# Three chained blocks on one core: gates, decays and sums of block 2 reordered, five norms taken by token columns, tokens chosen from PSUM

## The reference, cut to what matters

```python
def reference(x, ...):
    x = first_block(x, ...)    # mixer, then 16 experts that each choose 32 tokens
    x = second_block(x, ...)   # SSD and RG-LRU mixers, then a gated FFN with short convolutions
    return third_block(x, ...) # gated linear attention with windowed attention, then attention

def rmsnorm(x, w):             # twelve times in all
    return x * lax.rsqrt(jnp.mean(x * x, axis=-1, keepdims=True) + 1e-6) * w

# expert choice: each expert takes its 32 best tokens
aff = jax.nn.softmax(h @ w_router + b_router, axis=-1)
gate, idx = lax.top_k(jnp.swapaxes(aff, 1, 2), 32)

# block 2
y_a = ssd_mixer(u_z, u_xbc, u_dt, ...)   # decay = exp(segment sums); norm over each half of 1024 channels
y_b = rglru_mixer(u_ly, u_lx, ...)       # gates r, i from a block-diagonal product; scan over tokens
merged = g[:, :, 0] * (y_a @ w_proj_ssm) + g[:, :, 1] * (y_b @ w_proj_lru)
x = x + rmsnorm(merged @ w_out, mix_post_norm)
h = rmsnorm(x, ffn_pre_norm)
up = causal_dwconv(h @ w_ffn_up, ...)
x = x + rmsnorm((gelu(up_gate) * up_val) @ w_ffn_down, ffn_post_norm)
```

## Time and profile before

| what | value |
|---|---|
| three runs, median | 1859.84 us (1855.25 to 1861.47) |
| the profiled execution | 1862.03 us, its span 1860.1 us |
| TensorE busy | 1472.5 us (79%), 10438 matmul passes |
| VectorE, ScalarE, GpSimd busy | 720.2, 591.6, 35.9 us |
| mean granted TensorE clock | 0.903 of full |
| DMA | 573.55 MB, 308 GB/s over the span |
| the chain that ended last | TensorE 49%, DMA 41%, VectorE 7%, ScalarE 2% |

### The profile page before, as it was taken

The page is one execution under the profiler, slowest core; times in us unless marked ns, Lnnn a source line. Parts: engine busy times, 40 slices in busy tenths (PEclk is TensorE's granted clock), DMA queues, the critical chain, the costliest instruction groups (busy, mean ns, idle before and its releaser), DMA issues.

```text
span 1860.1 us, 25075 instructions
## 1 busy us (share of the span) xinstructions
PE 1472.5 (79%) x10438; PEld 1002.2 (54%) x10438; DVE 720.2 (39%) x1257; ACT 591.6 (32%) x1007; POOL 35.9 (2%) x40
## 2 busy tenths in 40 slices
PE   6999996566666565656656557999999999999997
PEld 4787941111111111111211113998998999999997
DVE  4457610000000000000000001987976998478765
ACT  6444510000000000000000002667576776465654
POOL 0000200000000000000000000000000000000201
PEclk9999898888778878787888888999999999999999
DMA  9566689999999999999999999556554555454330
GB/s 400 211 242 239 281 369 386 428 428 428 428 428 428 428 428 428 428 428 428 428 428 428 428 428 427 210 164 181 189 203 167 198 183 182 182 170 170 137 137 23
DMA packets 52978, 573.55 MB, mean 308 GB/s; under 512 B 4768, under 2 KB 15264, under 8 KB 16416
## 3 DMA queue, kind: packets, MB, share of 16 engines
q1 hardware_dynamic: 47296, 563.10, 74.5%
q10 hardware_dynamic: 5600, 9.28, 1.4%
HBM read 568.04 MB, written 4.33 MB: 308 GB/s over the span
## 4 chain that ended last, share of the span: by engine, by line
PE 49%; DMA 41%; DVE 7%; ACT 2%; issue 1%; SPq 0%; ACTq 0%; DVEq 0%
PE bank L1620 48%; DMA ring<-in_w_up 14%; DMA ring<-in_w_down 13%; DMA ring<-in_w_gate 13%; DVE ring_rounded L2376 2%; DVE work L735 1%; DMA ring<-in_dense 1%; DMA ring<-in_w_ada 1%; ACT work L2067 1%; DVE rstd L2316 1%; ACT weights_high_rounded L2067 1%; DVE ring_rounded L2387 0%; ACT L2067 0%; DVE work L726 0%; ACT squares L2067 0%
## 5 line engine op out<-in xcount | busy, mean ns | idle before, releaser
L1620 PE MATMUL bank<-ring,work 128*32 128x512 f32 x3008 | 480.4, 772 | 306.9 <-DMA ring<-in_w_up 125.6
L1620 PEld LDWEIGHTS bank<-ring,work 128*32 128x32 f32 x3008 | 93.1, 126 | 657.9 <-DMA ring<-in_w_up 207.7
L2067 ACT ACTIVATE work<-bank 128x512 f32<-128x512 f32 (+2 forms) x152 | 72.9, 492 | 1009.2 <-PE bank L1620 677.4
L2376 DVE TENSOR_TENSOR ring_rounded<-ring,weights_high_rounded 128x1024 fp32r<-128x1024 f32 x208 | 252.8, 1220 | 86.4 <-ACT weights_high_rounded L2067 86.3
L2067 ACT ACTIVATE weights_high_rounded<-ring 128x1024 fp32r<-128x1024 f32 x244 | 254.3, 1051 | 50.9 <-PE bank L1620 50.3
L2625 DVE TENSOR_TENSOR work<-work,bank 128x512 f32<-128x512 f32 x16 | 16.5, 1029 | 590.5 <-PE bank L1620 590.5
L1620 PE MATMUL bank<-h_high_rounded,weights_high_rounded 128*128 128x256 f32 x1264 | 192.1, 291 | 1.8 <-ACT h_high_rounded L2067 1.4
L1620 PE MATMUL bank<-h_high_rounded,ring_rounded 128*128 128x256 f32 x1264 | 174.3, 278 | 2.4 <-DVE ring_rounded L2387 2.4
L1620 PE MATMUL bank<-h_normed_rounded,weights_high_rounded 128*128 128x256 f32 x1264 | 176.1, 280 | 0.0
L1620 PEld LDWEIGHTS bank<-h_high_rounded,weights_high_rounded 128*128 128x128 f32 x1264 | 166.4, 191 | 12.9 <-issue 6.6
L1620 PEld LDWEIGHTS bank<-h_normed_rounded,weights_high_rounded 128*128 128x128 f32 x1264 | 160.9, 189 | 0.2
(11 more groups left out here) (259 smaller groups left out, 1221.3 us busy)
## 6 DMA issues: line engine op xcount, KB each, us to landing
ring<-in_w_down SPq DMA_DIRECT2D x64, 2048.0 KB, 16.2
ring<-in_w_gate SPq DMA_DIRECT2D x63, 2048.0 KB, 16.4
ring<-in_w_up SPq DMA_DIRECT2D x61, 2048.0 KB, 16.5
ring<-in_dense SPq DMA_DIRECT2D x60, 2048.0 KB, 8.3
ring<-in_w_ada SPq DMA_DIRECT2D x12, 2048.0 KB, 13.6
work<-in_w_up SPq DMA_DIRECT2D x3, 1024.0 KB, 14.8
bias_diagonals<-work SPq DMA_DIRECT2D x2, 1536.0 KB, 9.1
ring<-in_dense SPq DMA_DIRECT2D x2, 1024.0 KB, 18.6
```

Of the source, the lines that this page charges most:

```text
L1620: return nc.tensor.matmul(o, lhsT, rhs, start=start, stop=stop)
L2067: return nc.scalar.activation(o, i, f, **kw)
L2376: v.tensor_tensor(as_r(w), w, w_high[:, buffer, :], ALU.subtract).then_inc(s.w_low, 1)
```

## The change

Norms 2, 4, 6, 8 and 11 are summed by token columns: the squares are the stationary operand and two columns of ones move, so that a 128 x 4 result holds the sums of 256 tokens on partitions. The root and its reciprocal are taken of that; two matmuls with the identity spread the reciprocals to 128 x 256 in a bank, from where VectorE reads them. Token choice: the first round of the search reads the bank, the copy and the last replacement go, and the filler is 8 matmuls in place of 16, with one new one before the gather. `root_table` for norms 6, 8, 10 and 11 stands two units earlier. In block 2 the first gates wait for their own channels, `xdt_ready` is waited for at the first pair, the first two decays stand ahead of the recurrence's Exp, `masked(0)` ahead of a weight split; the gated norm's squares are added on VectorE and summed with 2 matmuls behind unit 4; the bias table is made behind norm 6, its copies stand before root 7, and its stores on SP behind one more round of loads. Semaphores that are no longer needed are merged.

```diff
+TOKEN_NORMS = {2: 7, 4: 4, 6: 6, 8: 6, 11: 6}
...
             def lru_gates(channels):
+                pe.wait_ge(s.conv_in, 3 * (CONV_UNITS.index(13) + channels[-1] + 1))
...
             in2(*range(2, 23))
-            pe.wait_ge(s.conv_in, 3 * len(CONV_UNITS))
...
-            pe.wait_ge(s.xdt_ready, 4)
             for u in range(27, IN2):
                 in2(u)
...
                 n = PAIR_AFTER[u]
+                if n == 0:
+                    pe.wait_ge(s.xdt_ready, 4)
...
-            for n in range(4):
+            for n in range(5):
                 unit2(L_LRU + n, lru, None if n else "lru")
-            pe.wait_ge(s.ya_sq, 1)
+            pe.wait_ge(s.ya_added, 1)
             for g in range(2):
-                for k in range(4):
-                    last = mm(B[4 + g][:, 0:SEQ], ones[:], SQ[:, 4 * g + k, :], k == 0, k == 3)
+                last = mm(B[4 + g][:, 0:SEQ], ones[:], SQ[:, 4 * g, :])
             last.then_inc(s.ya_sum, 1)
...
-                if n == 2:
-                    pe.wait_ge(s.start_in, 48)
-                    pe.wait_ge(s.ya_inv, 1)
-                    pe.wait_ge(s.toep_sb, 1)
-                    for kind in range(2):
-                        mm(B[4 + kind][:, 0:TOEP], REL_COPIES[0:REL_BUCKETS + 1, :],
...
-            added_sums(6)
-            awake_through_norm(6, B[6], 4, 4)
+            added_token_sums(6)
+            spread_roots(6, B[7], 0, 0)
+            pe.wait_ge(s.start_in, 48)
+            pe.wait_ge(s.ya_inv, 1)
+            pe.wait_ge(s.toep_sb, 1)
+            for kind in range(2):
+                mm(B[4 + kind][:, 0:TOEP], REL_COPIES[0:REL_BUCKETS + 1, :],
...
-            added_sums(8)
-            awake_through_norm(8, B[6], 4, 4)
+            added_token_sums(8)
+            spread_roots(8, B[5], 2, 4)
...
             in2(26)
+            def decay(n):
+                act.wait_ge(s.seg_ready, n + 1)
+                fn(SEG[:, n], SEG[:, n], ACT.Exp).then_inc(s.seg_exp, 1)
+
+            decay(0), decay(1)
+            in2(27)
             for k in range(KT):
                 last = fn(TH[:, k, :], TH[:, k, :], ACT.Exp, scale=LAMT[:, k:k + 1])
             last.then_inc(s.th_ready, 1)
-            in2(27)
...
-            decay(0), decay(1)
...
-                if n == KT - 2:
+                if n == KT - 4:
                     root_table(6)
             root(6)
             weight_high(D1_UNITS + L_UP - 1 + AHEAD2)
             raw_splits(2 * KT, HH_plain, par("ffn_pre"))
+            for kind in range(2):
+                act.wait_ge(s.toep_mm, kind + 1)
+                fn(TW[:, kind, 0:TOEP], B[4 + kind][:, 0:TOEP], ACT.Copy).then_inc(s.toep_sb, 1)
             root(7)
...
             scaled2(27)
+            masked(0)
             weight_low(27 + AHEAD2)
-            masked(0)
...
+            dve.wait_ge(s.ya_act, 1)
+            halves = SQ[:, :, :].rearrange("p (g h a) t -> p g h (a t)", g=2, h=2)
+            link(v.tensor_tensor(halves[:, :, 0], halves[:, :, 0], halves[:, :, 1], ALU.add))
+            v.tensor_tensor(halves[:, :, 0, 0:SEQ], halves[:, :, 0, 0:SEQ], halves[:, :, 0, SEQ:2 * SEQ], ALU.add).then_inc(s.ya_added, 1)
             dve.wait_ge(s.ya_sum, 1)
...
-            added_sums(11)
+            added_token_sums(11)
+            spread_roots(11, B[5], 0, 0)
...
-            rounds_before = (L_SSM + 4) // (RING * UNITS) + 1
+            rounds_before = (L_UP + 4) // (RING * UNITS) + 1
...
+            def token_sums(k, bank, first=False, last=False):
+
+                for t in range(TT):
+                    ins = mm(bank[:, 2 * t:2 * t + 2], SQ[:, k, t * P:(t + 1) * P], ones[:, 0:2], first and t == 0, last and t == TT - 1)
+                if last:
+                    ins.then_inc(s.norm_summed, 1)
...
+            def spread_roots(i, bank, before, behind):
+
+                stay_awake(before, bank)
+                pe.wait_ge(s.norm_inverted, i + 1)
+                for t in range(TT):
+                    last = mm(rstd_row(i)[:, t * P:(t + 1) * P], spread(TOKEN_ROOTS[:, 2 * t], 1, P), ident)
+                last.then_inc(s.norm_spread, 1)
+                stay_awake(behind, bank)
...
-            added_sums(2)
+            added_token_sums(2)
...
             last.then_inc(s.router_mm, 1)
-            awake_through_norm(2, B[7], 0, 3)
+            spread_roots(2, B[5], 0, 2)
...
             pe.wait_ge(s.aff_ready, 2)
-            stay_awake(16, B[7])
+            stay_awake(8, B[7])
             pe.wait_ge(s.topk_ready, 1)
...
+            stay_awake(1, B[5])
             pe.wait_ge(s.sel_ready, 1)
...
             for k in (0, 1):
-                mm(B[3][:, 0:SEQ], ones[:], SQ[:, k, :], k == 0, False)
+                token_sums(k, B[3], first=k == 0)
...
-            awake_through_norm(4, B[1], 6, 6)
+            spread_roots(4, B[1], 4, 6)
...
-                v.reciprocal(RS[:, i % 2, :], RS[:, i % 2, :]).then_inc(s.norm_inverted, 1)
-                dve.wait_ge(s.norm_inverted, i + 1)
+                root = TOKEN_ROOTS if i in TOKEN_NORMS else RS[:, i % 2, :]
+                v.reciprocal(root, root).then_inc(s.norm_inverted, 1)
+                if i in TOKEN_NORMS:
+                    dve.wait_ge(s.norm_spread, list(TOKEN_NORMS).index(i) + 1)
...
-            v.tensor_copy(at, B[7][0:EXPERTS, 0:SEQ]).then_inc(s.aff_ready, 1)
-            dve.wait_ge(s.aff_ready, 2)
+            left = B[7][0:EXPERTS, 0:SEQ]
             for r in range(CAP // 8):
                 best = VAL[0:EXPERTS, 8 * r:8 * r + 8]
-                link(v.max(best, at))
-                link(v.max_index(idx_u[:, 8 * r:8 * r + 8], best, at))
-                link(v.match_replace(at, best, at, -1.0))
+                link(v.max(best, left))
+                link(v.max_index(idx_u[:, 8 * r:8 * r + 8], best, left))
+                if r == 0:
+                    v.match_replace(at, best, left, -1.0).then_inc(s.aff_ready, 1)
+                    dve.wait_ge(s.aff_ready, 2)
+                elif r < CAP // 8 - 1:
+                    link(v.match_replace(at, best, left, -1.0))
+                left = at
```

More of the change, by code:

```diff
@@ L609, in scalar_block2 @@
             in2(26)
-            for k in range(KT):
-                last = fn(TH[:, k, :], TH[:, k, :], ACT.Exp, scale=LAMT[:, k:k + 1])
-            last.then_inc(s.th_ready, 1)
-            in2(27)
             def decay(n):
@@ L619, in scalar_block2 @@
             decay(0), decay(1)
+            in2(27)
+            for k in range(KT):
+                last = fn(TH[:, k, :], TH[:, k, :], ACT.Exp, scale=LAMT[:, k:k + 1])
+            last.then_inc(s.th_ready, 1)
             for u in range(28, IN2):
@@ L651, in scalar_block2 @@
                     act.wait_ge(s.ya_gated, 1)
[L652 removed]
+                    fn(flat(SQ), tiles(53, 8), ACT.Square).then_inc(s.ya_act, 1)
                 if n < 3:
@@ L668, in scalar_block2 @@
                     fn(TW[:, :, TOEP:TPITCH], ones[:, 0:2].unsqueeze(2), ACT.Copy).then_inc(s.toep_sb, 1)
-                    for kind in range(2):
-                        act.wait_ge(s.toep_mm, kind + 1)
-                        fn(TW[:, kind, 0:TOEP], B[4 + kind][:, 0:TOEP], ACT.Copy).then_inc(s.toep_sb, 1)
                 if n >= 2:
@@ L2119, in root @@
                 act.wait_ge(s.norm_summed, i + 1)
-                fn(RS[:, i % 2, :], B[bank][:, 0:SEQ], ACT.Sqrt, scale=1.0 / DM, bias=EPS_COL).then_inc(s.norm_root, 1)
+                sums, root = (B[bank][:, 0:2 * TT], TOKEN_ROOTS) if i in TOKEN_NORMS else (B[bank][:, 0:SEQ], RS[:, i % 2, :])
+                fn(root, sums, ACT.Sqrt, scale=1.0 / DM, bias=EPS_COL).then_inc(s.norm_root, 1)
             act.dma_start(params[:], d["params"]).then_inc(s.params_in, 16)
@@ L2188, in _ @@
                     act.wait_ge(s.start_in, 32)
-                    fn(tiles(60, 8), tiles(60, 8), ACT.Exp).then_inc(s.dmat_ready, 1)
+                    fn(tiles(60, 8), tiles(60, 8), ACT.Exp)
                 if 6 <= pu < 6 + HEADS1:
```

61 lines of the change are left out of this document (35 added, 26 removed).

## The result

| | before | changed |
|---|---|---|
| first comparison, median | 1857.55 us (1854.75 to 1861.47, 4 runs) | 1841.3 us (1840.39 to 1844.43, 4 runs) |
| a later comparison, median | 1858.64 us (11 runs) | 1845.2 us (1841.81 to 1846.93, 5 runs) |
| profiled execution (span) | 1862.03 us (1860.1) | 1840.39 us (1838.6) |
| TensorE busy, passes | 1472.5 us, 10438 | 1468.5 us, 10430 |
| VectorE, ScalarE busy | 720.2, 591.6 us | 711.0, 589.4 us |

The changed kernel is faster: the ratio is 0.9912 (95% interval 0.9895 to 0.993) in the first comparison and 0.9925 (0.991 to 0.994) in the second, so 16.3 and 13.4 us between medians, where 17.45 were forecast. Both medians of the changed kernel stand in the forecast range. The two profiles differ by more, 21.5 us of span, and part of that is not the change's, as the experiments show.

The account below looks back on a forecast made before the run. Expert weight transfers bound 289 to 1130 us, TensorE's work and 28 us of gaps 1132 to 1860; expert 0's start also counts. Terms sum to 17.45 us, giving 1842.4 us against the 1859.84 median, range 1836 to 1850.

Parts of the forecast that it names:

- token choice: Between router and expert 0: half the filler and a shorter search start the slot matmul, so expert 0, 2.0 us earlier.
- block 2 front: Block 2's gates, decays and pairs: waits removed and full clock at the gates, 7.3 us; bounds 3.2 and 8.
- gated norm, bias table: Before block 2's state projection: fewer TensorE sum passes, bias table moved out, part given back by VectorE; 3.2 us (1.5 to 4.5).
- The bound of 2.7: Token choice: at full clock the search, not the filler, would be last and the gain 2.7 us.
- the filler was needed: Rival, chance 0.06: with half the filler, gather and expert 0's first block run at half clock; 1845.7 us.
- (a): Block 2's first gates: TensorE's 2.80 us wait for the last taps of channel 7 goes.
- (c): Block 2's input projection: the 0.41 us wait for xdt before unit 27 moves to pair 0.
- (d): Block 2's pair 0: its 2.60 us wait for masked(0), which is ready some 4.5 us sooner against unit 28.
- (b): Block 2's 16 gate passes: 5.41 us at mostly half clock become 3.72 without the wait before them; 1.7 us gained.
- the clock falls from norm 6 on: Rival, chance 0.02: without filler in the norm TensorE's clock stays at 1.2 GHz; slower, 1866 us at 11 units.
- Tiles from a bank: VectorE's 40 tiles with a PSUM factor: no cost taken; rival, chance 0.06, 0.1 us more each, 1846 us.
- What would show it: Signs in the trace, among them 0.17 us reciprocals and 1.7 us from last squares to first tile at the five norms.

## Why the prediction was right, and where it was not

The forecast, 1842.4 us, stands between the two medians. The gain was 16.3 and 13.4 us by the medians; the steps of the trace, taken over all profiles with the same code, sum to 13.4, and 17.45 were forecast. So the mechanisms were mostly right and the sizes mostly too large, and that the first median came within 1.2 us of the forecast gain is in part the luck of the draw. By its own steps:

| term | forecast | steps, mean over profiles |
|---|---|---|
| token choice | 2.0 | 2.0 (57.9 against 59.9 with the old choice, three profiles) |
| norm 2 | 0.3 | -0.1 |
| norm 4 | 0.75 | 0.5 (3.85 against 4.39) |
| block 2 front | 7.3 | 6.0 (99.6 against 105.5; 5.4 without the one half clock of before) |
| gated norm, bias table | 3.2 | 2.1 (127.65 against 129.72) |
| norm 6 | 1.5 | 0.2 (36.1 against 36.3) |
| norm 8 | 1.2 | 1.1 to its first tile; behind it 0.4, one stretch in three profiles of the old form |
| norm 11 | 1.2 | 1.2 (0.7 the norm, 0.5 the root tables) |

*Token choice.* The filler was last, not the search, and 2.26 us went at the slots' matmul in the first pair of profiles. The bound of 2.7 "at full clock" also came true (6.28 us against 8.93). I had given the rival "the filler was needed" 0.06; the step from the slots to expert 0 is 0.2 to 3.2 us longer in the eight profiles with 8 matmuls, and the mean of 2.0 is what is left after it, with the uncertainty said above.

*Block 2's front.* (a), (c) and (d) came out at 2.96, 0.57 and 2.75 us in the first pair. The step that failed is (b): I read the half clock of 16 gate passes as the price of the wait before them and took 1.7 us. The wait stood in three profiles, the half clock behind it in one. A term that rests on one execution's clock row is not a term of the code. The new form also runs at two speeds, shown in the last section: 98.95 us from norm 4's first tile to pair 0 in five profiles and 100.05 in six.

*Gated norm.* As forecast, 3.3 us came off before the state projection and 1.5 were taken back by the low parts; the bias table gave 1.6 (7.26 to 5.6 us). Missed was a second give-back of 0.7 to 1.7 at the merged tiles. I followed VectorE to the low parts and stopped; its queue is still behind seven units later, since it needs 2.27 us per unit against 2.84 of TensorE.

*The norms.* Root and reciprocal of four values took 0.26 and 0.18 us, and norm 8 gained 1.11 of the 1.2. Norm 11 gained 0.7 by its form and 0.5 by the earlier root table, which I had put at nothing. At norm 4 the mechanism was right: the 8 passes of filler took 1.14 us at full clock, and 0.96 was gained of the 0.75 forecast; in four of ten profiles half clock took a part or all of it back. At norm 2 I had the router's passes ahead of the spread in the argument and still gave 0.3. At norm 6 the mechanism was right (the step from the output projection to its first tile went from 24.75 to 23.39 us at full clock), but I dropped the filler without a price. The rival that the clock falls from norm 6 on had 0.02 and was priced as a lasting fall, many units long; the clock does fall there in eight of nine profiles, but for one or two stretches, 1.0 to 2.6 us between norm 6's sums and unit 2. (By its own terms that rival gives 1867 us at 11 units, not 1866: 1859.84 less 17.45 and 11 times 2.26 more.)

*Tiles from a bank* cost nothing: 0.41 us for 256 columns, 0.33 from start to start. By the Trainium skill (VectorE: DVE Perf Modes, the section on the TRN2 errata) each would have been 65 ns longer. The trace doesn't agree: two tiles took 0.75 us with the factor in a bank and 0.76 with it in SBUF.

*What would show it.* The signs came, but for the size of one: from the start of norm 11's last sums to its first tile it took 1.98 to 2.50 us (3.09 before), where 1.7 were named. TensorE's gaps fell to 16 us, 12 less, while the stage fell by 18. The rest is TensorE's busy time: fewer passes and less half clock.

## What to carry to other kernels

Read a clock row as a draw, not as a constant: take a second profile of the same kernel before a half-clock stretch goes into a sum, and compare steps between landmarks rather than spans. Where work is taken from the engine that waits last (here 3.3 us of TensorE's sums), the gain is what the next engine's chain allows (1.1 us at best, 0.5 on the mean), and that chain has to be followed until it has caught up. Price filler before taking it out of a gap ahead of dense matmuls: at the gather 8 matmuls did better than 16, 4 or none by the ring's load, and at norm 6 two brought 1.3 us over none, both on few profiles.

## What the runs showed of the hardware

Clock losses came in portions: the granted clock lacked 1.7 us of full, or a multiple of it, wherever it fell but in the last stretch of each profile, and the 8.9 us between executions of the kernel before (1852.58 to 1861.5 us in 17 runs on one chip) are as much as five of them. The gather's 32 passes took 3.7 or 7.0 us, 48 passes of expert 0 5.36 or 7.05.

A unit of 24 rounded passes in block 2's input projection took 2.79 us in some executions and 2.86 in others, of the same code, and held it for the whole projection: the step from norm 4's first tile to the first gate is 71.34 to 71.37 us in five profiles of the new gates and 72.77 or 72.78 in six, and the units themselves ran at full granted clock in both. I found nothing in the trace that tells the two apart; in before it is hidden, since the wait for the taps takes it up (the idle time there was 2.80, 2.77 and, in the kernel with the front put back, 1.34 us). Its cause stays open.
